# A product-key expert layer whose value rows are gathered for two token blocks fewer and swept once as a whole table

## The reference, cut to what matters

```
q    = x1 @ w_pq, 8 heads x 2 halves;  sc = q . sub_keys        # 128 keys per half
s, i = top 16 of each half;  top, sel = top 16 of the 256 sums s[0] + s[1]
eidx = i[0]*128 + i[1]                                          # one of 16384 experts
g    = softmax(top)                                             # 16 per head
hid  = dot(x1, u_tab[eidx]);  a = g * gelu(hid)                 # 128 experts per frame
y    = LayerNorm(alpha*x1 + sum over 128 experts of a * v_tab[eidx])
```

## Time and profile before

| | us |
|---|---|
| median of three runs (1898.70 to 1900.74) | 1899.08 |
| span of the profiled execution | 1895.5 |
| VectorE busy | 1263.2 |
| TensorE busy (modelled ends) | 1601.3 |
| GpSimd busy | 1245.3 |
| ScalarE busy | 627.4 |

### The profile page before, as it was taken

The page is one execution under the profiler, slowest core; times in us unless marked ns, Lnnn a source line. Parts: engine busy times, 40 slices in busy tenths (PEclk is TensorE's granted clock), DMA queues, the critical chain, the costliest instruction groups (busy, mean ns, idle before and its releaser), DMA issues.

```text
span 1895.5 us, 20537 instructions
## 1 busy us (share of the span) xinstructions
PE 1601.3 (84%) x6192; PEld 881.4 (47%) x6192; DVE 1263.2 (67%) x2836; ACT 627.4 (33%) x1771; POOL 1245.3 (66%) x1199
## 2 busy tenths in 40 slices
PE   8999779879978698888898889998689877767877
PEld 7596445536435355355354465634436422222322
DVE  2379984576767755868587647589756897655543
ACT  1432561223237422232276222136522232222211
POOL 3027676576677755777777665677777777777771
PEclk9999999999989999999999998998899999999999
DMA  9899999999999999999999999999999999999995
GB/s 318 309 347 371 410 393 387 410 409 409 386 412 409 409 401 409 406 408 409 411 406 393 397 406 377 406 409 370 405 411 409 409 410 409 409 409 409 410 409 225
DMA packets 210197, 744.60 MB, mean 393 GB/s; under 512 B 24640, under 2 KB 29544, under 8 KB 209960
## 3 DMA queue, kind: packets, MB, share of 16 engines
q0 software_dynamic: 166720, 605.75, 80.9%
q1 hardware_dynamic: 43368, 137.53, 19.0%
HBM read 736.03 MB, written 7.75 MB: 392 GB/s over the span
## 4 chain that ended last, share of the span: by engine, by line
DMA 35%; PE 30%; POOL 20%; issue 9%; DVE 6%; ACT 1%; SPq 0%; DVEq 0%; ACTq 0%
DMA vbuf<-in_peer_v,idx 18%; PE acc L959 10%; POOL ubuf L1670 9%; POOL vbuf L1670 8%; DMA ubuf<-in_peer_u,idx 8%; PE mixer L667 5%; DMA held<-in_peer_u,idx 4%; PE mixer L833 2%; PE mixer L936 2%; DVE ubuf L1598 2%; PE mixer L683 2%; DMA wring<-in_c_k 1%; POOL wring L1670 1%; DMA held<-in_peer_v,idx 1%; POOL held L1670 1%
## 5 line engine op out<-in xcount | busy, mean ns | idle before, releaser
L959 PE MATMUL acc<-vbuf,diag 128*128 128x512 f32 x1308 | 644.5, 627 | 159.5 <-DMA vbuf<-in_peer_v,idx 154.6
L1670 POOL DMA_INDIRECT ubuf<-in_peer_u,idx x518 | 553.9, 1069 | 255.5 <-issue 138.4
L1670 POOL DMA_INDIRECT vbuf<-in_peer_v,idx x478 | 512.4, 1072 | 264.4 <-PE acc L959 133.0
L1598 DVE CUSTOM_DVE_ANT_0 ubuf<-ubuf,x 128x1024 f32<-128x1024 f32 x332 | 404.9, 1224 | 252.9 <-DMA ubuf<-in_peer_u,idx 249.7
L959 PEld LDWEIGHTS acc<-vbuf,diag 128*128 128x128 f32 x1308 | 236.7, 196 | 470.4 <-issue 429.0
L1598 DVE CUSTOM_DVE_ANT_0 ubuf<-ubuf,mixer 128x1024 f32<-128x1024 f32 x186 | 225.6, 1218 | 118.2 <-DMA ubuf<-in_peer_u,idx 81.9
L1200 ACT ACTIVATE act_h<-hid 128x4 f32<-128x4 f32 x144 | 29.5, 205 | 504.1 <-DVE hid L1598 503.4
L936 PEld LDWEIGHTS mixer<-stage,wring 128*128 128x128 f32 x1280 | 149.5, 193 | 17.4 <-issue 15.4
L936 PE MATMUL mixer<-stage,wring 128*128 128x128 f32 x1280 | 150.6, 276 | 0.7 <-DMA wring<-in_w_pq 0.6
L1229 ACT ACTIVATE diag<-ident,coef 128x128 f32<-128x128 f32 x392 | 138.4, 395 | 22.1 <-PE acc L959 18.1
L1610 DVE SCALAR_TENSOR_TENSOR y_acc<-vbuf,coef,y_acc 128x1024 f32<-128x1024 f32 x99 | 127.3, 1286 | 18.1 <-DMA vbuf<-in_peer_v,idx 16.0
(11 more groups left out here) (266 smaller groups left out, 1959.1 us busy)
## 6 DMA issues: line engine op xcount, KB each, us to landing
wring<-in_w_pq SPq DMA_DIRECT2D x80, 512.0 KB, 8.1
wring<-in_w_qk SPq DMA_DIRECT2D x66, 512.0 KB, 7.6
wring<-in_w_out SPq DMA_DIRECT2D x40, 512.0 KB, 7.5
wring<-in_w_v SPq DMA_DIRECT2D x20, 512.0 KB, 7.5
ubuf<-in_peer_u,idx POOLq DMA_INDIRECT x518, 13.0
vbuf<-in_peer_v,idx POOLq DMA_INDIRECT x478, 12.7
wring<-in_c_k SPq DMA_DIRECT2D x8, 512.0 KB, 6.9
wring<-in_c_v SPq DMA_DIRECT2D x8, 512.0 KB, 7.9
```

The costliest lines, as they stand in the source:

```text
L959: last = pe.matmul(sums[hf], diags[D_PLAN[n][0]], v_buf[b][:, hf * 512:(hf + 1) * 512], start=first, stop=last_one)
L1598: nc.vector.tensor_tensor_reduce(out=u, in0=u, in1=x, scale=1.0, scalar=0.0, op0=ALU.mult, op1=ALU.add, accum_out=hid[:, k % MARKS:k % MAR ...
L1670: pool.indirect_dma_start(buf, None, a[table], bass.IndirectOffsetOnAxis(ap=idx[p % 2][:, at:at + 1], axis=0)).then_inc(landed_, 16)
```

## The change

- `GATHERED = (0, 3, SMP)` and `DENSE = (1, 2)`. Blocks 1 and 2 gather u rows only. Their row numbers (high and low part), gains and `hid` are kept, and gelu and gains are applied once per block to 128x128 elements (lane `b`).
- Their v side is one pass over all of `v_tab`, lane `d`. For each of the 256 frames a matmul over its 128 slots multiplies a one-hot matrix of the low row part (`hot_j`) with one of the high row part scaled by the activations (`hot_i`), which gives how much of each expert the frame takes. VectorE makes both one-hot tiles four frames at a time, ScalarE scales one and copies the result out, TensorE multiplies. This is done in three chunks of high parts (54, 37 and 37 of 128), 64 groups of four frames each. Then each of the 128 tiles of `v_tab` (128 rows, 512 KB, SyncE's queue, six buffers) enters four 128x512 matmuls.
- Chunk 0 stands at slots 391 to 412, the tiles at 412 to 574, the other two chunks among the tiles.
- In blocks 3 and `SMP` every v row is added by VectorE; only block 0 still uses TensorE and diagonals. `x1` is read from SBUF there; the PSUM copies from slot 440 on are gone. The u and v buffers stay at six each.
- The preparation of blocks 2, 3 and `SMP` moves earlier (`STAGES`). The sample search runs over four heads for two copies, in place of eight.
- `HELD` is 3 in place of 4: one more `w_v` tile is streamed per block.

```diff
-    return ((0, 1), (1, 3), (3, 8)) if p == 0 else ((0, 4), (4, 8)) if p == SMP else ((0, 8),)
+    return ((0, 1), (1, 3), (3, 8)) if p == 0 else ((0, 4),) if p == SMP else ((0, 8),)
...
+GATHERED = (0, 3, SMP)
+DENSE = (1, 2)
...
-U_MORE, V_MORE = ((368, 1), (438, 2)), ((360, 3), (430, 3))
-D_MORE = ((432, 8),)
...
+    return part_of(k) == 0 and k >= 3 and (62 <= k < 122 or k % 3 != 2)
...
-BLOCK_1 = (5, 26), (26, 54), (54, 65), (65, 81), (70, 122)
-BLOCKS = (-30, 6), (6, 46), (46, 60), (60, 78), (66, 121)
+STAGES = {
+    1: ((5, 26), (26, 54), (54, 65), (65, 81), (70, 122)),
+    2: ((84, 104), (104, 140), (140, 156), (156, 176), (162, 246)),
+    3: ((176, 200), (200, 240), (240, 256), (256, 276), (268, 344)),
+    SMP: ((276, 300), (300, 350), (350, 364), (364, 382), (380, 450)),
+}
+SWEEP_FROM, SWEEP, SWEEP_TO = NBP * SLOTS - SLOTS + 7.0, 412.0, JSLOTS - 2.0
...
+CHUNKS = ((0, 54), (54, 91), (91, P))
+TOK = 4
+GROUPS_D = DBLK // TOK
+DRING_T = 6
+HOTS = 3
...
+    users += [("", 0, 0)] * 2
+    for n in range(P):
+        users.append(("v", n, 0))
+        for c, (lo, hi) in enumerate(CHUNKS[1:], 1):
+            first, last = hi - HOMES, lo - 2
+            if first <= n <= last:
+                a, b = ((n + d - first) * GROUPS_D // (last + 1 - first) for d in (0, 1))
+                users += [("g", c, k) for k in range(a, b)]
...
+                if g_ >= HOTS:
+                    dve.wait_ge(bank_done, BANK_AT[G_USERS[g_ - HOTS]] + 1)
+                nc.vector.tensor_tensor(hot_j[g_ % HOTS].rearrange("p (t n) -> p t n", n=P),
+                                        jig[:, 1, t0:t0 + TOK].unsqueeze(2).broadcast_to([P, TOK, P]),
+                                        iota[:, :].unsqueeze(1).broadcast_to([P, TOK, P]), ALU.is_equal)
+                hi3 = hot_i[g_ % HOTS][:, 0:TOK * w].rearrange("p (t n) -> p t n", n=w)
+                nc.vector.tensor_tensor(hi3, jig[:, 0, t0:t0 + TOK].unsqueeze(2).broadcast_to([P, TOK, w]),
+                                        iota[:, lo:hi].unsqueeze(1).broadcast_to([P, TOK, w]), ALU.is_equal).then_inc(hot_done, 1)
...
+                for t in range(TOK):
+                    cols = hot_i[g_ % HOTS][:, t * w:(t + 1) * w]
+                    last = nc.scalar.activation(cols, cols, ACT.Copy, scale=jig[:, 2, u[2] * TOK + t:u[2] * TOK + t + 1])
...
+                for t in range(TOK):
+                    last = pe.matmul(bank[:, t * w:(t + 1) * w], hot_j[g_ % HOTS][:, t * P:(t + 1) * P],
+                                     hot_i[g_ % HOTS][:, t * w:(t + 1) * w], start=True, stop=True)
...
+                pe.wait_ge(bank_out, BANK_AT["g", CHUNK_OF[n], GROUPS_D - 1] + 1)
+                pe.wait_ge(tile_in[n % DRING_T], 16 * (n // DRING_T + 1))
+                home, w = n % HOMES, tiles[n % DRING_T]
+                for q in range(len(DENSE)):
+                    for hf in range(2):
+                        last = pe.matmul(acc_d[q][hf], big[:, home * DBLK + q * P:home * DBLK + (q + 1) * P],
+                                         w[:, hf * 512:(hf + 1) * 512], start=False, stop=n == P - 1)
```

More of the change, by code:

```diff
@@ L116, in part_of, with end_of, has_row, row_no @@
     return min(k // SLOTS, NBP)
-def on_tensor(k):
[L121 to L137, removed]
-for _k in range(JSLOTS):
[L139 to L153, removed]
-    return plan
[L157 to L160, removed]
+def end_of(p):
+    return min((p + 1) * SLOTS, JSLOTS)
+def has_row(k):
+    return part_of(k) in GATHERED
+def row_no(k):
+    return k if k < SLOTS else k - len(DENSE) * SLOTS
+def on_tensor(k):
+    return part_of(k) == 0 and k >= 3 and (62 <= k < 122 or k % 3 != 2)
+ROWS = [k for k in range(JSLOTS) if has_row(k)]
+PE_COUNT, DV_COUNT = [0], [0]
+for _k in range(JSLOTS):
+    PE_COUNT.append(PE_COUNT[-1] + (has_row(_k) and on_tensor(_k)))
+    DV_COUNT.append(DV_COUNT[-1] + (has_row(_k) and not on_tensor(_k)))
+def ring_plan(jobs, size):
+    plan, had, last = {}, [0] * size, [None] * size
+    for n, k in enumerate(jobs):
+        b = n % size
+        plan[k] = (b, last[b], had[b])
+        last[b], had[b] = k, had[b] + 1
+    return plan
+U_PLAN = ring_plan(range(JSLOTS), URING)
+V_PLAN = ring_plan(ROWS, VRING)
+D_PLAN = ring_plan(range(PE_COUNT[JSLOTS]), DRING)
 def nkeys(p):
@@ new lines, with bank_plan @@
+USERS = sweep_users()
+G_USERS = [u for u in USERS if u[0] == "g"]
+G_INDEX = {u: n for n, u in enumerate(G_USERS)}
+BANKED = [u for u in USERS if u[0] in ("t", "g", "r")]
+BANK_AT = {u: n for n, u in enumerate(BANKED)}
+CHUNK_OF = [next(c for c, (lo, hi) in enumerate(CHUNKS) if lo <= n < hi) for n in range(P)]
+FEW = BANK_AT["g", 1, 0]
+def bank_plan():
+    plan, last = [], [None] * 4
+    for m in range(len(BANKED)):
+        bank = m % 2 if m < FEW else (m - FEW + 2) % 4
+        plan.append((bank, last[bank]))
+        last[bank] = m
+    return plan
@@ new lines, with home_pieces, sweep_marks @@
+BANK_PLAN = bank_plan()
+D_STEPS = len(USERS) + OUT_LAG
+def home_pieces(c):
+    lo, hi = CHUNKS[c]
+    out = []
+    while lo < hi:
+        n = min(hi - lo, HOMES - lo % HOMES)
+        out.append((lo, lo % HOMES, n))
+        lo += n
+    return out
+def sweep_marks():
+    before = USERS.index(("v", 0, 0))
+    out = [SWEEP_FROM + (k + 0.5) * (SWEEP - SWEEP_FROM) / before for k in range(before)]
+    cost = [{"v": 3.5, "g": 1.0, "r": 1.0}[u[0]] for u in USERS[before:]] + [1.0] * OUT_LAG
+    at, total = 0.0, sum(cost)
+    for c in cost:
+        out.append(SWEEP + (at + 0.5 * c) * (SWEEP_TO - SWEEP) / total)
+        at += c
+    return out
@@ L653, in x_tensor @@
             wait(pe, t_out, T_BASE[p])
-            wait(pe, y_done, p - 2)
             for t in range(MATS):
@@ L1260, in x_vector, with e_scalar @@
+        def e_scalar(act, _):
+            for t in range(4):
+                if t == 1:
+                    for q in range(len(DENSE)):
+                        act.wait_ge(lnd_v, q + 1)
+                        nc.scalar.activation(rstd[:, q:q + 1], mvd[q][:, 1:2], ACT.Sqrt, bias=eps[:, 0:1]).then_inc(lnd_r, 1)
+                yield
         def x_vector(dve, p, chain):
```

540 lines of the change are left out of this document (363 added, 177 removed).

## The result

The changed kernel takes 2009.97 us (median of 4 runs, 2006.27 to 2012.12) against 1898.89 us for the kernel before in the same series: ratio 1.0587, 95% interval 1.057 to 1.0604. It was forecast at 1878 us, faster; it is 5.9% slower.

What follows compares the result with a forecast made beforehand. The prediction took the kernel before to be bound by bytes, at about 410 GB/s. Its stretches summed as 533 + 590 + 751 = 1874 us, plus 3.6 from span to median: 1878 us, range 1790 to 1960.

Steps and rivals of the forecast that it cites:

- The middle, 590 us: Slots 128 to 383, u gathers only: 590 us, before 816; slot 384 beginning after 1180 would show the forecast wrong.
- Two stages turn VectorE-bound: In slots 128 to 383, VectorE's work sets block 3's attention at 87 us and the sample's at 106 us.
- 87 + 106 + 371 + 18: Slots 128 to 383: two attention stages, bytes of the other 166 slots, two output projections; 582 us, taken as 590.
- Chunk 0, 114 us: Slots 391 to 412: VectorE's sum of 110 us sets the stretch, above ScalarE's 97; taken as 114 us.
- The sweep, 590 us: Slot 412 to the last u product: 445 loads need 570 us, plus 20 for GpSimd's gathers; VectorE has 514.
- TensorE is no bound: Slots 128 to 383: without its v rows TensorE has 710 - 385 = 325 us listed.
- twice that would fit: From slot 384 on: TensorE needs 225 us for tiles and 84 us for small matmuls, and twice that would fit.
- Slots 0 to 127, 533 us: Stretch ending at slot 128: block 0 as before, 5 more loads add 6 us to 526.8, giving 533.
- 384 to 390 and the tail: Slots before chunk 0 take 12 us; the tail, with 12 v rows and two dense blocks normalized, takes 35 us.
- The second: Rival 2, whole kernel: stages don't overlap and VectorE's waits are lost; about 1970 us, half of it 1920; chance 25%.
- The third: Rival 3, whole kernel: buffers carry enough, so each stretch takes its larger total; 1740 us, halfway 1810; chance 17%.
- The first: Rival 1, from slot 412: GpSimd's gathers become the bound, deciding from 1.5 us each; about 1970 us; chance 12%.

Runs made afterwards that it cites:

- e6: e3 with the six idle v buffers lent to u gathers from slot 152 to 383; 1937.84 us, ratio 1.0212 to the kernel before.
- e11: e6 with block 3's search in slots 264 to 299 in place of 268 to 343; 1927.76 us, ratio 1.0158 to the kernel before.
- e15: e11 with block 2's search in slots 162 to 203 in place of 162 to 245; 1916.13 us, ratio 1.0088 to the kernel before.
- e3: The changed kernel with four PSUM banks in chunk 0 in place of two and a fourth pair of one-hot buffers; 1980.67 us, ratio 1.0001.
- e13: e6 with `hot_j` made in chunk 0 only, old buffer contents used in chunks 1 and 2; 1919.93 us, ratio 1.0113.
- e1: The changed kernel with one added 128x512 identity matmul per slot in slots 146 to 390; 2029.06 us, ratio 1.023.
- e9: The changed kernel with one added 128x128 identity matmul per slot in slots 146 to 390; 2006.44 us, ratio 1.0592.
- e10: e6 without the second dense block's two 128x512 matmuls for 127 of the 128 v table tiles; 1941.49 us, ratio 1.0229.
- e7: e6 with two in three of block 3's v rows on TensorE, six banks in chunk 0, two afterwards, three one-hot buffers; 2057.77 us, ratio 1.0841.
- the second pair of profiles: The kernel before and the changed kernel, both unchanged, run again in the series of e5 and e6; 1900.44 and 2010.05 us.
- e8: The changed kernel with one added 128x512 identity matmul behind each of chunk 0's 64 groups; 2071.63 us, ratio 1.0922.
- e2: The changed kernel with two added 128x512 identity matmuls behind each of chunk 0's 64 groups; 2047.24 us, ratio 1.0322.
- e5: The changed kernel with four PSUM banks in chunk 0 in place of two, still three one-hot buffers; 1978.32 us, ratio 1.0429.

## Why the prediction was wrong

1. *The middle, 590 us: failed, 55 us.* Slot 384 begins at 1192 us, behind the 1180 that the prediction named as its sign of being wrong. The step that failed is "Two stages turn VectorE-bound", with "87 + 106 + 371 + 18". It gave each of these stages VectorE's sum as its length and let the other 166 slots run at the full rate of bytes. Block 3's attention took 94 (VectorE full, its sum was 7 short), the sample's 130: VectorE busy for the 106 forecast and idle for 25 more, 21 of them waiting for scores. The other slots took 421 against 371 + 18 and 8 of reserve. Shown in its place: 20 us are six u buffers being too few to carry bytes over a stage boundary while six others stand empty (e6), and 14 and 17 us (10 and 12 in the totals) are the two searches placed beside the attentions (e11, e15). With all three the middle takes 601 us, 11 from the forecast. The charge for output projections, two of 9 us, was too low too: three fall into the middle, since block 2's was moved there, and they wait 37.3 us in the row above and 47.8 us in e15, the longest wait that is left; how much of that reaches the end was not tested by itself.
2. *Chunk 0, 114 us: failed, 43 us.* The step "ScalarE has 64 x 1.4 + 7 = 97 us, so VectorE sets it" left out TensorE and the buffers between the engines. ScalarE was at 80 us and no limit. The four matmuls of a group cost 1.7 us (111.5/64 in e3) and not 0.44, twice as much by the misread records and twice again by the clock of 0.51; with two banks and three one-hot buffers each engine waits in turn for the others, 43.4 us on VectorE. Freed of that (e3, e6), the stretch takes 111.8, and VectorE's 110.1 us is exactly the sum that was forecast. The sum was right and its condition, that the buffers let it be reached, was not looked at. That the stretch can come down to it is luck: TensorE, which the sum left out, is full for 111.5 us there.
3. *The sweep, 590 us: held, at 596, for another reason than given.* Bytes need 570; the 20 us on top were put down to GpSimd and go away with VectorE's one-hots among the tiles (e13), while GpSimd waits 118 us for VectorE (e6). That both are 20 is luck.
4. *"TensorE is no bound", "twice that would fit": the price was wrong by two and the outcome just held.* The earlier trace rows list TensorE as busy for 88% and 87% of the first two windows, and "no engine pressed" took that for a fault of the listing; at 0.87 us the 388 matmuls of the earlier trace rows are 338 of the 385 us listed, so the listing was near the truth. In the middle it is busy for 471 us and not the 325 of the subtraction, at a clock of 0.78 in place of 0.95 and with work brought forward; e1 and e9 find no price for that. In the sweep, at 0.87 us the tiles take 128 x 4 x 0.87 = 445 us, and with the small matmuls TensorE is busy for 570 of 594 (e6). It fitted with 4% to spare: taking 221 us of matmuls away gains nothing (e10), adding 83 rows x 2 x 0.87 = 144 us, most of it behind slot 412, makes slots 412 to 511 100 us longer (e7).
5. *Slots 0 to 127, 533 us: missed by 14, most of it not the change's.* 6 of the 14 us lie ahead of slot 0 (127.8 against 121.6 us), where the two kernels move the same 38 MB. In the second pair of profiles slot 128 stands at 539.9 against 529.9, 10 us later in place of the 6 forecast, and the stretch moved 416.0 x 394 = 163.9 MB against 406.7 x 396 = 161.1, that is 5 or 6 loads: near the "5 loads".
6. *384 to 390 and the tail: 9 and 5 us too low.* The 12 us took the buffers to be full on arrival. Not tested by itself.
7. *Rivals.* The second, stages that don't overlap, is nearest to what happened. It gave 227 us for the two attention stages (224 measured) and 605 for the sweep (596), but 129 for chunk 0; at 1970 us it fell 40 us short. The third assumed the buffers to carry enough; e6 shows that this was worth 20 us. The first is out: gathers took 1.19 to 1.20 us over the kernel and 1.27 to 1.41 where chunks 1 and 2 lie between the tiles (e6, slots 450 to 539), under the 1.5 from which it was to decide, and there VectorE is busy for 97%, 93% and 100% of slots 450 to 489, 490 to 511 and 512 to 539. In chunk 0 the u gathers took 1.68 us, but GpSimd waited for VectorE for 91 of the 157 us.

The range ended at 1960, short even of rival 2's own 1970, to which a chance of 25% was given; and that sum had chunk 0 at only 15 us more. What should have widened it is a stretch with VectorE forecast at 96% and ScalarE at 85% that passes its work through TensorE and two banks.

## What to carry to other kernels

When a kernel is bound by bytes at full rate, waits on the other engines can be free, as the 54 us for output projections were here; once bytes are taken away, they have to be paid, so price a changed stage as the longest chain between engines, with its buffers, and not as the longest sum. Find out how many records one instruction leaves before dividing a time by a count: eight records of fp32 matmuls were four. And a busy share of 96% does not name the bound: take the work away and see, as e10 did.

## What was not expected of the hardware

- The granted clock does not follow TensorE's listed busy time. In chunk 0 it stood at 0.51 with TensorE busy 118.6 of 156.6 us and 111.5 of 111.8, and at 0.50 with 209.6 of 209.6 (e8); with one more 128x512 matmul per group it was 1.00 and the same stretch, with more work than in e8, took 164.1 us (e2). The kinds of matmul differ between these cases, and the runs do not say what decides.
- Less work lowers the clock and hides its own gain: in e10 the sweep's matmul records fell by 25% and TensorE's busy time by 23%, though the ones left out are the long ones and would be 39% of it at an unchanged clock.
- One chip ran the kernel before in 1982 us and the others in 1897 to 1900. On that chip e3 tied with it (1980.67 us, 1.0001), while e5, which has only part of e3's edit and took 1978.32 us, was 4.3% slower than it on another: how much slower a variant is can depend on the chip. On it slots 0 to 127, which the variants walk as the kernel before does, took 433 to 443 us against 416 to 420 elsewhere, and the sweep 593 to 599 us as elsewhere; the kernel before ran there at a granted clock of 0.92 to 0.93 in place of about 0.96. There is no trace of the kernel before from that chip, and the cause is open.
